# Both token tiles' expert selections in one VectorE instruction, and all gather evictions on VectorE, in a decoder with a mixture of experts

## The reference

```
g_prob = softmax(hs @ w_rg + b_rg);  g_p, g_idx = top_k(g_prob, 1)
e_in   = expert logits of the chosen group (8 of 32);  e_top, e_idx = top_k(e_in, 2)
w      = g_p * softmax(e_top)            # weights of the two experts of a token
hg, hu = hs @ w_gate[e], hs @ w_up[e]    # 32 experts, 1024 -> 256
act    = silu(hg) * hu * combine[..., None]
x      = x + sum over e of act @ w_down[e]    # 256 -> 1024
```

## Time and profile before

| | us |
|---|---|
| median of 3 runs | 787.36 (785.94 to 788.03) |
| the profiled execution | 786.42 |
| its span, first to last instruction | 784.6 |
| loop over the experts, first layer | about 168 to 391 |
| loop over the experts, second layer | about 550 to 784 |

### The profile page before, as it was taken

How to read it: one execution, slowest core, us unless ns; L and a number is a source line. 1 busy time by engine, 2 the same in 40 slices (tenths; PEclk the granted TensorE clock), 3 DMA queues, 4 the chain that set the end, 5 groups by cost and what they waited for, 6 DMA issues and landing times.

```text
span 784.6 us, 12425 instructions
## 1 busy us (share of the span) xinstructions
PE 673.1 (86%) x4720; PEld 372.6 (47%) x4721; DVE 298.8 (38%) x671; ACT 144.5 (18%) x370; POOL 8.5 (1%) x18
## 2 busy tenths in 40 slices
PE   8999999989878988585899999999879689794776
PEld 5444556565444553341344455647444445452432
DVE  0346652164233533231425366324332335341323
ACT  3114431311101001001031245222101010010010
POOL 0000100000000000000020000000000000000000
PEclk9999999999989998797999999999989799997879
DMA  8798429429998999995999242454699589999965
GB/s 305 234 375 320 65 108 373 165 84 406 420 417 330 425 419 421 422 419 225 366 362 387 112 160 108 174 231 185 267 373 420 231 324 424 420 421 420 419 248 216
DMA packets 52949, 239.31 MB, mean 305 GB/s; under 512 B 7760, under 2 KB 8048, under 8 KB 29328
## 3 DMA queue, kind: packets, MB, share of 16 engines
q1 hardware_dynamic: 52416, 238.09, 76.6%
q0 software_dynamic: 464, 0.47, 0.9%
HBM read 237.49 MB, written 1.05 MB: 304 GB/s over the span
## 4 chain that ended last, share of the span: by engine, by line
PE 64%; DMA 19%; issue 7%; DVE 5%; DVEq 2%; SPq 2%; ACT 1%; ACTq 0%
PE bank L1165 20%; DMA wbuf<-in_w_down 18%; PE bank L1350 9%; PE bank L1262 7%; PE bank L1293 7%; PE bank L1318 5%; PE bank L1362 5%; PE bank L1329 2%; SPq L359 1%; PE bank L1242 1%; PE bank L1185 1%; DMA wbuf<-in_w_in 1%; PE bank L1222 1%; PE bank L1269 1%; PE bank L1196 1%
## 5 line engine op out<-in xcount | busy, mean ns | idle before, releaser
L1165 PE MATMUL bank<-wbuf,hTbuf 128*128 128x512 f32 x384 | 170.2, 599 | 2.8 <-DMA wbuf<-in_w_in 2.4
L1318 PE MATMUL bank<-wbuf,qkT 128*32 128x256 f32 x2048 | 113.8, 380 | 2.4 <-DVE qkT L860 2.4
L1165 PEld LDWEIGHTS bank<-wbuf,hTbuf 128*128 128x128 f32 x384 | 72.2, 191 | 90.0 <-issue 87.2
L1350 PE MATMUL bank<-wbuf,qkT 128*32 128x512 f32 x512 | 70.2, 694 | 48.0 <-DMA wbuf<-in_w_down 40.4
L1293 PE MATMUL bank<-qkT,xn 128*128 128x128 f32 x512 | 71.3, 305 | 27.0 <-DVEq L831 17.3
L1318 PEld LDWEIGHTS bank<-wbuf,qkT 128*32 128x32 f32 x2048 | 65.2, 110 | 54.4 <-issue 10.6
L1293 PEld LDWEIGHTS bank<-qkT,xn 128*128 128x128 f32 x512 | 68.2, 218 | 34.5 <-DVEq L831 18.2
L893 DVE TENSOR_TENSOR x_sb<-x_sb,bank 128x512 f32<-128x512 f32 x72 | 49.5, 688 | 50.9 <-PE bank L1362 50.9
L1350 PEld LDWEIGHTS bank<-wbuf,qkT 128*32 128x32 f32 x512 | 16.8, 125 | 91.7 <-issue 80.9
L1262 PE MATMUL bank<-wbuf,hTbuf 128*128 128x512 f32 x128 | 56.0, 593 | 0.0
L583 ACT ACTIVATE qkT<-bank,g2T 128x128 f32<-128x128 f32 x64 | 18.3, 368 | 135.8 <-PE bank L1293 135.8
(11 more groups left out here) (213 smaller groups left out, 597.8 us busy)
## 6 DMA issues: line engine op xcount, KB each, us to landing
wbuf<-in_w_gate SPq DMA_DIRECT2D x64, 1024.0 KB, 13.5
wbuf<-in_w_up SPq DMA_DIRECT2D x64, 1024.0 KB, 17.8
wbuf<-in_w_down SPq DMA_DIRECT2D x56, 1024.0 KB, 12.2
wbuf<-in_w_in SPq DMA_DIRECT2D x24, 1024.0 KB, 14.5
wbuf<-in_w_out SPq DMA_DIRECT2D x8, 1024.0 KB, 6.8
wbuf<-in_w_down SPq DMA_DIRECT2D x16, 512.0 KB, 7.9
x_sb<-in_x SPq DMA_DIRECT2D x2, 512.0 KB, 5.7
out<-x_sb SPq DMA_DIRECT2D x2, 512.0 KB, 2.6
```

What stands on the lines that cost most here:

```text
L1165: last = MM(ps[PROJ_BANK[i][t]][:, :], hT[:, k, t * P:(t + 1) * P], block_rows(i, k), start=(k == 0), stop=(k == KC - 1))
L1318: last = MM(ps[bank][j * SLOTS:(j + 1) * SLOTS, 0:FF], hgT[:, k, j * SLOTS:(j + 1) * SLOTS], halves[:, at[j], k, :], start=(k == 0), stop= ...
L1350: last = MM(ps[banks[h]][j * SLOTS:(j + 1) * SLOTS, :], src[:, c, j * SLOTS:(j + 1) * SLOTS], at[j][:, c * D + h * HALF:c * D + (h + 1) * ...
```

## The change

VectorE's selections take both token tiles in one instruction (a 4-dimensional pattern; the slot numbers 1 to 32 are read with a step of zero for tiles and lanes). `columns` is gone: `following` copies both tiles' columns at once, and a further round subtracts directly from `pos` and reads the weights in place. `gather_copy` is on VectorE alone, one instruction for each bank, and the semaphores are now `hg0` and `hg1`. VectorE's loop becomes 60 instructions smaller and ScalarE's 24.

```diff
@@ -258,7 +258,7 @@
         rt_first, rt_second, rt_total = sem("rt_first"), sem("rt_second"), sem("rt_total")
         pos_ps, total_ps, routed = sem("pos_ps"), sem("total_ps"), sem("routed")
 
-        STEPS = ["sel_ready", "selw_ready", "gathered0", "gathered1", "selwT_ps", "hg_d", "hg_a", "selwT_out", "gu_ps", "gate_exp",
+        STEPS = ["sel_ready", "selw_ready", "gathered0", "gathered1", "selwT_ps", "hg0", "hg1", "selwT_out", "gu_ps", "gate_exp",
                  "act_out", "actT_ps", "actT_out", "dn0_ps", "dn1_ps", "y_d", "y_a", "sc00_ps", "sc01_ps", "sc10_ps", "sc11_ps"]
         first = {n: sem(n) for n in STEPS}
         more = {n: sem("more_" + n) for n in STEPS}
@@ -577,13 +577,6 @@
                 nc.scalar.copy(hT[:, 4:8, t * P:(t + 1) * P],
                                ps[OT_BANK[t][1]][:, :].rearrange("p (k c) -> p k c", k=4)).then_inc(oT_a, 1)
 
-            def gather_copy(s, n, dst):
-                act.wait_ge(s["gathered1"], n)
-                for k in range(4):
-                    last = nc.scalar.activation(dst[:, 4 + k, :], ps[1][:, k * P:(k + 1) * P], ACT.Copy,
-                                                scale=g2T[:, 4 + k:5 + k])
-                last.then_inc(s["hg_a"], 1)
-
             def weights_copy(s, n, dst, half):
                 act.wait_ge(s["selwT_ps"], n)
                 nc.scalar.copy(dst.rearrange("p t s -> p (t s)"), ps[SELW_BANK][:, half]).then_inc(s["selwT_out"], 1)
@@ -603,7 +596,6 @@
                 n = act.snap(g + l * SETS + 1)
 
                 def further(m, r):
-                    gather_copy(more, m, hgT_more)
                     weights_copy(more, m, selwT_more, more_half)
                     gate(more, m, MORE_GU)
                     with act.If(most <= r * SLOTS + SLOTS):
@@ -614,7 +606,6 @@
                         y_copy(more, m, MORE_DN[1], y_more)
 
                 def following():
-                    gather_copy(first, act.snap(n + 1), hgT)
                     weights_copy(first, act.snap(n + 1), selwT2[1 - parity], first_half)
 
                 act.wait_ge(routed, l + 1)
@@ -705,7 +696,6 @@
                 nc.scalar.activation(r4[:, 1], r4[:, 0], ACT.Exp).then_inc(rt_exp, 1)
                 act.wait_ge(rt_diff, 2 * l + 2)
                 nc.scalar.activation(rs[:, 5, :], rs[:, 4, :], ACT.Exp).then_inc(rt_exp, 1)
-                gather_copy(first, l * SETS + 1, hgT)
                 weights_copy(first, l * SETS + 1, selwT2[0], first_half)
                 with act.Fori(0, SETS // 2) as pair:
                     for parity in range(2):
@@ -821,44 +811,40 @@
                 V.tensor_copy(hT[:, 0:4, t * P:(t + 1) * P],
                               ps[OT_BANK[t][0]][:, :].rearrange("p (k c) -> p k c", k=4)).then_inc(oT_d, 1)
 
-            slots_shape = [P, LANES, SLOTS]
-
-            def select_slots(s, rank, sel):
-                for t in range(TT):
-                    V.tensor_tensor(sel[:, t, :].rearrange("p (j s) -> p j s", j=LANES),
-                                    cst[:, C_IOTA:C_REV].rearrange("p (j s) -> p j s", j=LANES),
-                                    rank[t].unsqueeze(2).broadcast_to(slots_shape), ALU.is_equal)
+            def selection(ap):
+                return ap.rearrange("p t (j s) -> p t j s", j=LANES)
+
+            def each_slot(ap):
+                return ap.unsqueeze(3).broadcast_to([P, TT, LANES, SLOTS])
+
+            iota = cst[:, C_IOTA:C_IOTA + SLOTS].unsqueeze(1).unsqueeze(1).broadcast_to([P, TT, LANES, SLOTS])
+
+            def select_weights(s, weight, sel, selw):
+                V.tensor_tensor(selection(selw), selection(sel), each_slot(weight), ALU.mult)
+                gap().then_inc(s["selw_ready"], 1)
+
+            def select(s, rank, weight, sel, selw):
+                V.tensor_tensor(selection(sel), iota, each_slot(rank), ALU.is_equal)
                 gap().then_inc(s["sel_ready"], 1)
-
-            def select_weights(s, weight, sel, selw):
-                for t in range(TT):
-                    V.tensor_tensor(selw[:, t, :].rearrange("p (j s) -> p j s", j=LANES),
-                                    sel[:, t, :].rearrange("p (j s) -> p j s", j=LANES),
-                                    weight[t].unsqueeze(2).broadcast_to(slots_shape), ALU.mult)
-                gap().then_inc(s["selw_ready"], 1)
+                select_weights(s, weight, sel, selw)
+
+            def select_more(at, r):
+                V.tensor_tensor(posg[:, :, :], pos[:, :, at],
+                                cst[:, bass.ds(r + C_OFF, 1)].unsqueeze(2).broadcast_to([P, TT, LANES]), ALU.subtract)
+                gap()
+                select(more, posg[:, :, :], wgt[:, :, at], sel_more, selw_more)
 
             def columns_of(g):
                 kept = dve.value_load(which[0:1, bass.ds(SETS - g, 1)], min_val=int(BIG) - SETS + 1, max_val=int(BIG))
-                return (int(BIG) - kept) * LANES
-
-            def columns(at):
-                for t in range(TT):
-                    V.tensor_copy(posg[:, t, :], pos[:, t, bass.ds(at, LANES)])
-                    V.tensor_copy(wgg[:, t, :], wgt[:, t, bass.ds(at, LANES)])
-                gap()
-
-            def select(s, r, sel, selw):
-                if r is not None:
-                    V.tensor_tensor(posg[:, :, :], posg[:, :, :],
-                                    cst[:, bass.ds(r + C_OFF, 1)].unsqueeze(2).broadcast_to([P, TT, LANES]), ALU.subtract)
-                    gap()
-                select_slots(s, [posg[:, t, :] for t in range(TT)], sel)
-                select_weights(s, [wgg[:, t, :] for t in range(TT)], sel, selw)
+                return bass.ds(dve.snap((int(BIG) - kept) * LANES), LANES)
 
             def gather_copy(s, n, dst):
                 dve.wait_ge(s["gathered0"], n)
                 V.tensor_tensor(dst[:, 0:4, :], ps[0][:, :].rearrange("p (k s) -> p k s", k=4),
-                                g2T[:, 0:4].unsqueeze(2).broadcast_to([P, 4, P]), ALU.mult).then_inc(s["hg_d"], 1)
+                                g2T[:, 0:4].unsqueeze(2).broadcast_to([P, 4, P]), ALU.mult).then_inc(s["hg0"], 1)
+                dve.wait_ge(s["gathered1"], n)
+                V.tensor_tensor(dst[:, 4:8, :], ps[1][:, :].rearrange("p (k s) -> p k s", k=4),
+                                g2T[:, 4:8].unsqueeze(2).broadcast_to([P, 4, P]), ALU.mult).then_inc(s["hg1"], 1)
 
             def sigmoid(s, n):
                 dve.wait_ge(s["gate_exp"], n)
@@ -909,13 +895,15 @@
                         y_copy(more, m, MORE_DN[0], y_more)
                         into_x(more, m)
                         gap().then_inc(x_more, 1)
-                        columns(columns_of(g))
-                        select(more, r + 1, sel_more, selw_more)
+                        select_more(columns_of(g), r + 1)
 
                 def following():
-                    columns(columns_of(g + 1))
+                    at = columns_of(g + 1)
+                    V.tensor_copy(posg[:, :, :], pos[:, :, at])
+                    V.tensor_copy(wgg[:, :, :], wgt[:, :, at])
+                    gap()
                     dve.wait_ge(first["selwT_ps"], n)
-                    select(first, None, sel, selw)
+                    select(first, posg[:, :, :], wgg[:, :, :], sel, selw)
 
                 if parity == 0:
                     following()
@@ -923,8 +911,7 @@
                     with dve.If(pair < SETS // 2 - 1):
                         following()
                 with dve.If(most > SLOTS):
-                    columns(columns_of(g))
-                    select(more, 1, sel_more, selw_more)
+                    select_more(columns_of(g), 1)
                 sigmoid(first, n)
                 activate(first, ps[FIRST_GATE][:, 0:FF], (ps[FIRST_UP][:, 0:FF], dve.snap(n * LANES)), act_sb)
                 with dve.If(most > SLOTS):
@@ -1091,7 +1078,8 @@
                 V.scalar_tensor_tensor(pos[:, :, 0:EXPERTS], ps[5][:, 0:2 * EXPERTS].rearrange("p (t e) -> p t e", t=TT), 1.0,
                                        asg[:, 0:TT, :], ALU.add, ALU.mult)
                 gap()
-                select_slots(first, [pos[:, t, 0:LANES] for t in range(TT)], sel)
+                V.tensor_tensor(selection(sel), iota, each_slot(pos[:, :, 0:LANES]), ALU.is_equal)
+                gap().then_inc(first["sel_ready"], 1)
                 dve.wait_ge(total_ps, l + 1)
                 V.tensor_reduce(cntf[:, :], ps[6][:, 0:EXPERTS].rearrange("p (g j) -> p g j", j=LANES),
                                 AX.X, ALU.max)
@@ -1109,7 +1097,7 @@
                     V.scalar_tensor_tensor(wgt[:, t, 0:EXPERTS], oh2[:, t, :], rs[:, 6, t:t + 1], wgt[:, t, 0:EXPERTS],
                                            ALU.mult, ALU.add)
                 gap()
-                select_weights(first, [wgt[:, t, 0:LANES] for t in range(TT)], sel, selw)
+                select_weights(first, wgt[:, :, 0:LANES], sel, selw)
 
                 square = [P, LATE, LATE]
```

(4 more changed lines are left out.)

## The result

The changed kernel took **753.35 us** (median of 4 runs, 750.33 to 755.24) against 787.69 for the kernel before in the same series: ratio 0.956, 95% interval 0.953 to 0.960. The gain is 34 us. A repetition in another series gave 754.25 (5 runs), ratio 0.959 (0.957 to 0.961).

The account below looks back on a forecast made before the run. Weight loads were taken to bound the expert loops, running dry behind each third set. Gains of 4.3, 10.3 and 0.3 us (shorter loop starts) sum to 14.9, giving 772.4 us; range 769 to 784.

Parts of the forecast that it names:

- What bounds it, and what the stops are.: Expert loops: loads set the pace but run dry behind each third set, as VectorE stops 5.4 to 5.6 us loading code.
- How much VectorE keeps.: VectorE holds four 128-instruction pages (32 KB); after the change three pages and one ahead fit, so all six returns' stops go.
- So the gate loads go out 7.7 earlier ... Dry time bounds the gain: 4.3.: First layer, third set: wait, slowed clock and entry let gate loads go 7.7 us earlier; gain limited to 4.3 dry.
- So 10.3 there.: Second layer, third set: 11.0 of 13.3 us dry time goes, less 0.7 for the second eviction.
- Evictions.: Second eviction on VectorE adds 0.7 us in the second layer's dry stretch, nothing elsewhere; removing ScalarE's four gives nothing.
- Other returns ... they are exchanged for waiting on down. Nothing.: At the loops' other returns, TensorE's 17.3 us of selection waits lie where loads run at 421 GB/s: no gain.
- Dry time bounds the gain.: Both loops: only time taken out of dry stretches (4.3 and 13.3 us by bytes) or short tails can shorten them.
- Rival 1: VectorE holds three pages or drops the loop's head; returns still stop 5.4 to 5.6 us: 783.9, chance 0.13.
- Rivals 2 and 3: TensorE's wait goes, another release holds gate loads: 787, chance 0.06; VectorE's eviction delays y's copy: 791.5, chance 0.05.

Follow-up runs that it names:

- experiment 1: The kernel before, its work unchanged, with 78 never executed instructions ahead of each layer's VectorE code, so its loops lie in three pages: 752.51 us.
- experiment 2: The changed kernel with never executed instructions ahead of the first layer's VectorE loop: 62 (loops over four pages) 786.82 us; 40 (three pages) 755.37 us.
- experiment 5: The changed kernel with idle GpSimd looping over 632 instructions beside the first layer's experts: 4 turns 769.71 us, 8 turns 783.70; control of 162 instructions 754.55.
- experiment 4: The changed kernel with three (first layer) or four (second) extra VectorE reciprocals at each return of the loop, stops without code loading: 763.51 us.
- experiment 3: The changed kernel with the second bank's eviction back on ScalarE, VectorE's loops still in three pages: 755.15 us.
- experiments 4 to 6: experiment 4, experiment 5, and the changed kernel with GpSimd's 632-instruction loop, 4 turns, beside the second layer's loop instead: 764.35 us.
- experiment 7: The changed kernel with extra VectorE reciprocals at each return and three turns of GpSimd's 632-instruction loop in both layers: 766.57, 769.46, 908.19 and 3825.68 us.

## Why the forecast was right in kind and half the size

- **What bounds it, and what the stops are.** Right. The stops are code loading: stops and packets come and go with the place of the code alone (experiments 1 and 2). In experiment 2 the second stops stand where the prediction's pages end, at instructions 320 and 832.
- **How much VectorE keeps.** The Trainium skill (Runtime: NRT & Kernel Launch, "Instruction fetch mechanics") is borne out in its 32 KiB, four of these packets. Four pages of 128 fit every run, but the stops alone don't prove them: each of VectorE's loops that returned without a stop also lies in two blocks of 256 that begin at 64 + 256k, and each one that stopped in three. That a loop of 276 still misses its head, as the prediction had it from that section, would follow for them only if a third block were fetched ahead. What speaks for pieces of 128 is the packets. They have 8 KB and come singly: 215.8, 220.8, 244.4, 268.7 and 278.0 behind the first return before, five for a turn where three blocks of 256 would make six. And GpSimd, whose jumps in experiment 5 span some 126 instructions, stops at every one. A loop over four pages of 128 in only two blocks of 256 would decide it and wasn't run.
- **"So the gate loads go out 7.7 earlier ... Dry time bounds the gain: 4.3."** The wait, the cold clock and the gather behind it went as worked out; the stop alone is worth 2.7 in experiment 4, against 4.3 forecast.
- **"So 10.3 there."** 9.3 in experiment 4, whose wait was 0.9 short there. The two terms that were worked out in detail came to 12.0 by the loops of that run (9.7 by the medians) against 14.6.
- **Evictions.** 0.68 stands on the chain where it was put; experiment 3 sees no cost from it. ScalarE's shorter work gave nothing that shows (experiment 1 has the old work and the whole gain).
- **"Other returns ... they are exchanged for waiting on down. Nothing."** This is the step that failed. It took 421 GB/s for the limit of what the loads can do, and so missed that the packets of each return are paid for even where no load is late in being issued. The loops had 16 and 15 packets of 8 KB more than after the change. At the measured 0.53 to 0.59 us that is 8.5 to 9.4 in the first layer; at 0.42, 6.3 in the second. With the stops: 11.2 to 12.1 of 14.1, and 15.6 of 19.9.
- **"Dry time bounds the gain."** The bound was wrong as well, for the same reason: it counts bytes over all sixteen engines, and the end of a load isn't a matter of bytes but of the slowest engine.'s 421 GB/s to 360 hid that one engine was up to 7 us behind. An estimate from the kernel before's own trace comes near the whole: dry time 4.3 and lag 8.1 make 12.4 of the first layer's 14.1; in the second layer 13.3 of dry time, of which 1.3 stays (28 us at 402 GB/s), and 7.5 of lag make 19.5 of 19.9.
- **The rivals.** None came. Rival 1 (the stops stay) would have left 47 packets, and experiment 2's four pages show no gain at all rather than its 3.5, though with a second stop at each return that the rival hadn't. Rivals 2 and 3 fell with the filled stretches and with experiment 3.
- **What the range lacked.** It took in how much of a stop is on the path, and not that a stop has a second price on another resource.

Open: some 2 to 3 us of the first layer's gain and 4 of the second's are not covered by the sum of experiments 4 to 6. Part of it can be the scatter of single executions and the short copy of the stops. Stops and packets may also cost more together than each alone; experiment 7 was to tell and didn't. Why a packet sets the engine back by up to 1.0 us, when it takes 0.31 to 0.34 itself, and how the engine that fetches is chosen, isn't shown.

## What to carry to other kernels

Before you shorten work in a loop, see where its code lies: count its instruction packets by queue and look for "issue" behind the jump back. If the loop covers one page more than the engine keeps, move it (some never-executed instructions ahead of it are enough) and measure that alone, or a change that only moves it will be credited with the gain. And where loads bind, compare the time at which a whole group of loads is there with the pace of the bytes: a stretch at a DMA share of 0.06 behind a stretch at 1.0 is one engine that everyone waits for.

## What was unexpected of the hardware

- An instruction packet of 8 KB costs the loads of 1 MB 0.42 to 0.59 us, and the costs add up: 54 of them cost 31.8 us. By bytes alone 8 KB at 421 GB/s would be 0.02 us, and on one of sixteen engines 0.31. The price lasts because the engine that lags doesn't catch up while the loads are dense (8.8 us of lag from 305 to 374 in experiment 5); in the dry stretch of the kernel before it did (2.3 at 233, 0.0 at 243).
- Such a fetch takes the engine that waits for it longer where the loads are dense: GpSimd's stops before each page were about 4.9 us there (5.9 at its own return) and 2.0 to 2.3 at the start of the loops, before the loads fill the engines. VectorE's were 5.4 to 5.6.
- 62 instructions that are never executed made the changed kernel 33 us slower, 78 in each layer made the kernel before 35 us faster (787.9 and 752.51 in one series).
